# Triangular inverses of a chunked RWKV-7 scan: 64x64 matrices in two passes, or their diagonal 32x32 blocks in one

## The chip, the cores and the metric

The kernel runs on one NeuronCore of a Trainium2 chip. The metric is the device time in microseconds (us) of one execution, as the median of several. TensorE is called PE for its products and PEld for its weight loads, VectorE is DVE, ScalarE is ACT, GpSimd is POOL, SyncE is SP. All operands of the part that is changed are float32.

## The reference

Two layers on a sequence of 256 tokens with 1024 features: an RWKV-7 time mix, then a sparse attention, each followed by a squared-ReLU MLP. The change touches only the recurrence of the time mix:

```
def wkv7_scan(r, w, k, v, a, b):
    """S_t = S_{t-1} diag(w_t) + (S_{t-1} a_t) b_t^T + v_t k_t^T ;  y_t = S_t r_t."""
    def step(S, inp):
        r_t, w_t, k_t, v_t, a_t, b_t = inp
        sa = jnp.einsum('bhij,bhj->bhi', S, a_t)
        S = S * w_t[:, :, None, :] + sa[..., None] * b_t[:, :, None, :] + v_t[..., None] * k_t[:, :, None, :]
        return S, jnp.einsum('bhij,bhj->bhi', S, r_t)
```

There are 16 heads of 64 features. The kernel does the recurrence in 4 chunks of 64 tokens. In a chunk the values `u_t = S_{t-1} a_t` depend on one another through a strictly lower triangular 64x64 matrix N (entry s,t is the product of a_s and b_t, with the decays in both), so that they are found with the inverse of (I - N). For 16 heads and 4 chunks that is 64 inverses of 64x64 matrices.

## The kernel before, in words

Everything is in one block per engine, written out by hand; each engine runs its instructions in the order of the code, and semaphores (`inv_pe0`, `inv_dve0`, `inv_act0`, `inv_pool0` and the same with 1) tie them together. The weights of the linears stream from HBM through a ring of four slots (`raw`), are split into a high and a low part by ACT (L1120) and DVE (L1526), and are multiplied by PE in `unit_mm` (L451).

The part around the change is this:

- PE ends the linear "v" (`linear8`, L620), transposes V into `ps` (L625) and the third chunk of BK (`b_k(2)`, L609). ACT copies the first half of the transposed V into `UV` (L1277) and then `BKT` (L1267), DVE the other half (L1701).
- The inverses follow. A pair of heads lies on the 128 partitions, one head on each half (`at(e)`), so the 64 matrices are 32 pairs. They are done in two passes (`NPAIR`) of two streams (s = 0 and 1) of 8 pairs (`NP_`); a stream's 8 pairs of 64x64 matrices are 128 partitions by 512 columns, one PSUM bank, and while one stream's result is copied, PE works on the other stream.
- In a pass, N comes from a product of AR and BK (`lower_products`, L658); ACT copies it to `Lr`; DVE masks its 16x16 diagonal blocks (L1737), turns them over in blocks of 32x32 (L1740) and adds the identity (L1742). POOL masks out of `Lr` what lies between the 16x16 blocks of a 32x32 block (`E32`) and between the two 32x32 blocks (`E64`, L2132).
- Then `times` (L667) makes one product for each matrix on 64x64 tiles of the PE array: sq1, sq2, add2, sq3, add3, add4 build the inverse of the 16x16 blocks as (I + N)(I + N^2)(I + N^4)(I + N^8); m32a and m32b join them to inverses of 32x32 blocks, m64a and m64b those to the 64x64 inverse `Rinv`. ACT copies the products that are used as they are (L1284), DVE adds the others to the running product (`add_to_product`, L1729) and turns over what becomes the next left factor (`turn_over`, L1732).
- While DVE prepares sq1, PE runs products whose result nobody reads (`idle_products`, L675: 4 before each stream's sq1, 5 at the end of the last pass). Then come `g_products` (L644), which DVE masks into `Gs` (L1711), and the recurrence over the four chunks, in which `Rinv` is the left factor of L815.

Of the kernel before, what the change touches and what calls it, by code (L numbers as in the profile page):

```python
# [8 lines left out]
P = 128  # L9
# [10 lines left out]
SUB = 16  # L20
LD, LI, LG = 64, 64, 160
# [19 lines left out]
def constants():  # L41
# [3 lines left out]
    t = np.arange(C)[None, :]  # L45
    same = (s // SUB) == (t // SUB)
    same32 = (s // (2 * SUB)) == (t // (2 * SUB))
    tt = np.arange(C)[None, :]
    cols = {
# [46 lines left out]
for _n, _w in (("ident", P), ("mean", P), ("pair", P), ("center", P), ("gmask", 2 * C), ("lmask16", C), ("lmask32", C),  # L96
               ("lmask64", C), ("eye64", C), ("hsel", 3 * H - 2), ("chunk", T),
               ("dist", P * TT * (TT + 1) // 2), ("adc", TT * H * 16), ("unit", P), ("shift", P), ("last", 2)):
    CONST_AT[_n] = (_o, _w)
    _o += _w  # L100
# [3 lines left out]
def rwkv_nsa_trunk(nc, t, out):  # L104
# [79 lines left out]
    LT = [place(f"LT{n}", [P, NP_, C], off(12 + n, 4096)) for n in range(2)]  # L184
    E32 = [place(f"E32{n}", [P, NP_, C], off(14 + n)) for n in range(2)]
    E64 = [place(f"E64{n}", [P, NP_, C], off(14 + n, 4096)) for n in range(2)]

    INV = {"L": 1, "sq1": 2, "sq2": 3, "add2": 4, "sq3": 5, "add3": 6, "add4": 7, "m32a": 8, "m32b": 9,  # L190
           "m64a": 10, "m64b": 11}
    NINV, NDVE, NACT, NPOOL = 11, 13, 5, 2
    Lr = [place(f"Lr{n}", [P, NP_, C], off(6, 2048 * n)) for n in range(2)]
# [126 lines left out]
    with ctx:  # L320
# [99 lines left out]
        def _(pe):  # L420
# [201 lines left out]
            pe.wait_ge(ev_act, EV0["v"] + 4)  # L622
            for q in range(TT):
                for k in range(FT):
                    last = nc.tensor.transpose(ps[:, 2 * q + k // 4, (k % 4) * P:(k % 4 + 1) * P],  # L625
                                               V[:, k, q * P:(q + 1) * P], cc("ident"))
                last.then_inc(sem("vT"), 1)
            pe.wait_ge(sem("bkt_act"), 1)
            b_k(2)

            pe.wait_ge(sem("ar_ready"), 2)

# [15 lines left out]
            def inv_bank(s, pair, name):  # L648
                return 4 * s + (NINV * pair + INV[name] - 1) % 4

            def lower_products(s, pair):

                p0 = (2 * pair + s) * NP_
                bank = inv_bank(s, pair, "L")
                for p in range(NP_):
                    k, c = (p0 + p) // NCH, p % NCH
                    for e in range(2):
                        last = mm(ps[at(e), bank, p * C:(p + 1) * C], AR[at(e), k, c, 0, :], BK[at(e), k, c, 0, :],  # L658
                                  start=True, stop=True)
                last.then_inc(sem(f"inv_pe{s}"), 1)  # L660

            def times(s, pair, name, lhs, which):

                bank = inv_bank(s, pair, name)
                for p in range(NP_):
                    for e in range(2):
                        last = mm(ps[at(e), bank, p * C:(p + 1) * C], lhs[s][at(e), p, :], DP[s][at(e), p, which, :],  # L667
                                  start=True, stop=True)
                last.then_inc(sem(f"inv_pe{s}"), 1)


# [5 lines left out]
            both = range(2)  # L677
            for pair in range(NPAIR):

                def dve_did(s, n):  # L680
# [1535 lines left out]
```

## Time and profile before

| | |
|---|---|
| time, median of 3 runs | 781.61 us (779.17, 781.61, 781.89) |
| span of the profiled execution, first to last instruction | 774.2 us |
| what lies around the span (median less span) | 7.4 us |
| PE busy | 745.7 us, 96% of the span, 7876 matmul records |
| PEld busy | 700.5 us, 90% |
| DVE busy | 521.3 us, 67% |
| ACT busy | 380.7 us, 49% |
| POOL busy | 71.4 us, 9% |
| mean granted clock of TensorE | 0.991 |

The profile gives no time of its own for the profiled execution beside its span. A float32 product is two records of PE and two of PEld (16 products of `times` are 32 records). Where the chain of waits puts the end on an engine, the time is that engine's; busy time elsewhere costs nothing by itself. A matmul record holds the whole way of its data through the array, so that records of a stream overlap; what a stream takes per record is its length, less one record's time, through the number of records.

### The profile page before, as it was taken

The page shows a single profiled execution, that of the slowest core. Times are in us where ns is not written, and L with a number is a line of the kernel's source. Part 1 is how long each engine was busy: PE and PEld are TensorE (multiplying, and loading weights), DVE is VectorE, ACT ScalarE, POOL GpSimd, SP SyncE. Part 2 cuts the span into 40 slices and gives each one's busy share as a digit, 9 for nine tenths or more (in the row PEclk, how much of TensorE's full clock was granted, in tenths as well). Part 3 has the DMA queues.
Part 4 walks back from the last instruction along what each step waited for, and adds up shares of the span by engine and source line. Part 5 has one row for each costly group of instructions (what it writes and reads, how often), then busy time and mean ns, then how long its engine had stood idle before and what let it go on. Part 6 is the DMA issues. An engine that isn't in the chain of part 4 may idle for free.

```text
span 774.2 us, 18656 instructions
## 1 busy us (share of the span) xinstructions
PE 745.7 (96%) x7876; PEld 700.5 (90%) x7876; DVE 521.3 (67%) x742; ACT 380.7 (49%) x584; POOL 71.4 (9%) x52
## 2 busy tenths in 40 slices
PE   8999999998999999999999999989999999999997
PEld 6988888998878999999999989866579999999997
DVE  4896986776453788785555678686857977764441
ACT  6657453121443645544444435767866544443441
POOL 0000005190130000000000010024320000000000
PEclk9999999999999999999999999998999999999999
DMA  9954330000111589967666554400045665676651
GB/s 294 273 172 130 108 110 3 5 3 2 57 56 45 164 216 250 241 193 221 197 195 194 170 164 115 159 1 1 1 139 164 193 209 178 204 212 194 192 164 54
DMA packets 110893, 109.23 MB, mean 141 GB/s; under 512 B 7120, under 2 KB 109776, under 8 KB 110704
## 3 DMA queue, kind: packets, MB, share of 16 engines
q1 hardware_dynamic: 110832, 108.34, 47.1%
q8 instruction: 47, 0.77, 0.4%
q14 instruction: 14, 0.11, 0.0%
HBM read 107.28 MB, written 1.05 MB: 140 GB/s over the span
## 4 chain that ended last, share of the span: by engine, by line
PE 83%; DVE 8%; ACT 3%; SPq 2%; DMA 1%; issue 1%; POOL 1%; ACTq 0%; DVEq 0%; POOLq 0%
PE ps L451 63%; PE ps L667 4%; DVE SB L2053 1%; DMA raw<-in_rwkv_w_in 1%; DVE Gs L1711 1%; PE ps L815 1%; ACT SB L1458 1%; PE ps L764 1%; PE ps L566 1%; PE ps L978 1%; DVE nmx L2059 1%; PE ps L758 1%; DVE LT L1737 1%; PE ps L549 1%; POOL t L2122 1%
## 5 line engine op out<-in xcount | busy, mean ns | idle before, releaser
L1526 DVE TENSOR_TENSOR wlo<-raw,whi 128x1024 fp32r<-128x1024 f32 x188 | 226.1, 1225 | 88.4 <-ACT whi L1120 86.1
L1120 ACT ACTIVATE whi<-raw 128x1024 fp32r<-128x1024 f32 x124 | 130.4, 1059 | 127.8 <-PE ps L451 122.4
L451 PE MATMUL ps<-xh,whi 128*128 128x256 f32 x896 | 178.6, 281 | 2.6 <-DVE xl L2081 1.0
L451 PE MATMUL ps<-xl,whi 128*128 128x256 f32 x896 | 175.7, 278 | 0.0
L451 PE MATMUL ps<-xh,wlo 128*128 128x256 f32 x896 | 175.6, 278 | 0.0
L451 PEld LDWEIGHTS ps<-xh,whi 128*128 128x128 f32 x896 | 135.7, 188 | 6.7 <-issue 4.1
L451 PEld LDWEIGHTS ps<-xl,whi 128*128 128x128 f32 x896 | 135.5, 188 | 0.0
L451 PEld LDWEIGHTS ps<-xh,wlo 128*128 128x128 f32 x896 | 135.4, 188 | 0.0
L1355 ACT ACTIVATE whi<-raw 128x1024 fp32r<-128x1024 f32 x64 | 68.0, 1063 | 78.0 <-PE ps L451 59.4
L451 PE MATMUL ps<-hh,whi 128*128 128x256 f32 x512 | 99.8, 276 | 0.0
L451 PE MATMUL ps<-hh,wlo 128*128 128x256 f32 x512 | 99.8, 276 | 0.0
L451 PE MATMUL ps<-hl,whi 128*128 128x256 f32 x512 | 99.8, 276 | 0.0
L451 PEld LDWEIGHTS ps<-hh,whi 128*128 128x128 f32 x512 | 77.1, 188 | 0.0
L451 PEld LDWEIGHTS ps<-hh,wlo 128*128 128x128 f32 x512 | 77.0, 188 | 0.0
L451 PEld LDWEIGHTS ps<-hl,whi 128*128 128x128 f32 x512 | 77.0, 188 | 0.0
L1863 DVE SCALAR_TENSOR_TENSOR rl<-ps,ri 128x512 f32<-128x512 f32 x32 | 22.1, 691 | 30.3 <-PE ps L451 29.9
L667 PEld LDWEIGHTS ps<-DP,LT 64*64 64x64 f32 x1024 | 30.7, 135 | 3.7 <-DVE DP L1742 2.5
L667 PE MATMUL ps<-DP,LT 64*64 64x64 f32 x1024 | 31.8, 219 | 1.8 <-DVE DP L1729 0.9
L2175 POOL TENSOR_TENSOR SB<-SB,cof 128x512 f32<-128x512 f32 (+1 forms) x16 | 24.4, 1523 | 80.0 <-DVE cof L2075 79.9
L1562 DVE TENSOR_TENSOR h<-h,ps 128x512 f32<-128x512 f32 x16 | 11.0, 688 | 29.8 <-PE ps L451 27.0
L1284 ACT ACTIVATE DP<-ps 128x512 f32<-128x512 f32 x16 | 9.6, 597 | 35.8 <-PE ps L667 35.8
L1866 DVE TENSOR_TENSOR s<-rl 128x512 f32<-128x512 f32 x32 | 22.2, 692 | 1.1
(309 smaller groups left out, 988.0 us busy)
## 6 DMA issues: line engine op xcount, KB each, us to landing
raw<-in_mlp_w SPq DMA_DIRECT2D x128, 512.0 KB, 4.4
raw<-in_rwkv_w_in SPq DMA_DIRECT2D x24, 512.0 KB, 5.0
raw<-in_nsa_w_in SPq DMA_DIRECT2D x20, 512.0 KB, 4.5
raw<-in_rwkv_w_out SPq DMA_DIRECT2D x8, 512.0 KB, 3.5
raw<-in_nsa_w_out SPq DMA_DIRECT2D x8, 512.0 KB, 3.5
cw<-in_nsa_cmp_w SPq DMA_DIRECT2D x4, 512.0 KB, 9.4
cst<-in_consts SPq DMA_DIRECT2D x1, 1047.0 KB, 11.2
xtok<-in_x SPq DMA_DIRECT2D x2, 512.0 KB, 4.3
```

The source lines that it names most:

```text
L451: last = mm(ps[:, bank0 + m, 0:T], w[:, slot, c0:c0 + P], x_[:, kk, :], start=(kk == 0 and n == 0), stop=(kk == ktiles - 1 and n == 2))
L549: last = mm(ps[:, 4 + 2 * (k % 2) + i, 0:T], lup[half, k * P:(k + 1) * P], hwa[half, :], start=True, stop=True)
L566: last = mm(ps[0:width, bank, 0:T], ldown[:, k, c0:c0 + width], mixg[:, k, :], start=(k == 0), stop=(k == FT - 1))
L667: last = mm(ps[at(e), bank, p * C:(p + 1) * C], lhs[s][at(e), p, :], DP[s][at(e), p, which, :], start=True, stop=True)
L1120: A(whi[:, s, :], raw[:, s, :], ACT.Copy).then_inc(hi_ready, 1)
L1284: A(dst, ps[:, bank, :].rearrange("p (k n) -> p k n", n=C), ACT.Copy).then_inc(sem(f"inv_act{s}"), 1)
L1355: A(whi[:, 2 * gg + j, :], raw[:, 2 * gg + j, :], ACT.Copy).then_inc(hi_ready, 1)
L1526: v.tensor_tensor(wlo[:, slot, :], raw[:, slot, :], whi[:, slot, :].bitcast(f32), ALU.subtract)\
L1562: v.tensor_tensor(h[:, 2 * g:2 * g + 2, :], h[:, 2 * g:2 * g + 2, :], ps[:, 2 * (g % 2):2 * (g % 2) + 2, 0:T], ALU.add).then_inc(ev_dve, 1)
L1863: v.scalar_tensor_tensor(rl[:, gg, :, :], ps[:, 2 * gg:2 * gg + 2, 0:T], 0.0, normal(2), ALU.max, ALU.mult)\
L1866: v.tensor_tensor(s2[:, gg, :, :], rl[:, gg, :, :], rl[:, gg, :, :], ALU.mult).then_inc(sem("s2_ready"), 1)
L2175: g.tensor_tensor(x, x, cof[:, q, b, 4 * j:4 * j + 4].unsqueeze(2).broadcast_to([P, 4, w]), ALU.mult)\
```

## The change

Each 64x64 matrix is no longer kept whole. Of a matrix only the two 32x32 blocks on its diagonal go through the steps up to m32b; the block below the diagonal (`F`) is made by a product of its own and is only used in m64a. The two heads of a pair have four diagonal blocks, one on each quarter of the 128 partitions. A stream is now 16 pairs (`NP_`) of 32 columns, again 128 partitions by 512 columns and one bank, and two streams hold all 32 pairs, so there is one pass.

- `times` makes four products of 32x32 for a pair where it made two of 64x64. m64a and m64b are two products for a pair (`moves`).
- A product of BK and AR gives the transposed matrix (`U`), so that DVE masks both orientations straight out of PSUM (`inv_first`) and the first turning-over is gone. `E64` and POOL's mask for it are gone.
- `Rinv` is put together from its parts: ACT copies the upper left block and m64b of the first head, DVE the lower right block and m64b of the second, POOL writes the zeros.
- The first stream's L, U and F come before the transposes of V. PE writes the third BK chunk's transposes to banks 0 and 1, and ACT's queue takes the first stream's copies between the others. `idle_products` stay only at the end (4 of them).

```diff
-        "lmask16": (s > t) & same,
-        "lmask32": (s > t) & ~same & same32,
-        "lmask64": (s > t) & ~same32,
-        "eye64": s == t,
+        "lmask16": (r > j) & same,
+        "umask16": (r < j) & same,
+        "lmask32": (r > j) & ~same,
+        "eye32": r == j,
...
-    NP_ = 8
-    NPAIR = FT * NCH // NP_ // 2
-    DP = [place(f"DP{n}", [P, NP_, 2, C], off(12 + n)) for n in range(2)]
...
-    NINV, NDVE, NACT, NPOOL = 11, 13, 5, 2
-    Lr = [place(f"Lr{n}", [P, NP_, C], off(6, 2048 * n)) for n in range(2)]
+    NP_ = FT * NCH // 2
+
+    DP = [place(f"DP{n}", [P, 2, NP_, Q], off(12 + n)) for n in range(2)]
+    LT = [place(f"LT{n}", [P, NP_, Q], off(12 + n, 4096)) for n in range(2)]
+    E32 = [place(f"E32{n}", [P, NP_, Q], off(14 + n)) for n in range(2)]
+    Lr = [place(f"Lr{n}", [P, NP_, Q], off(14 + n, 2048)) for n in range(2)]
+    F64 = [place(f"F64{n}", [P, NP_, Q], off(14 + n, 4096)) for n in range(2)]
+
+
+    INV = {"L": 1, "U": 2, "F": 3, "sq1": 4, "sq2": 5, "add2": 6, "sq3": 7, "add3": 8, "add4": 9, "m32a": 10, "m32b": 11,
+           "m64a": 12, "m64b": 13}
+    INV_ACT = {"L": 1, "F": 2, "sq1": 3, "sq2": 4, "m32a": 5, "own": 7, "m64a": 8, "m64b": 9}
+    INV_DVE = {"lower": 1, "upper": 2, "first": 3, "sq1T": 4, "sq2T": 5, "add2": 6, "sq3T": 7, "add3": 8, "add4": 9, "add4T": 10,
+               "m32b": 11, "m32bT": 12, "own": 14, "m64b": 15}
...
+            def inv_bank(s, name):
+                return 4 * (1 - s) + (INV[name] + 2 * s - 1) % 4
+
+            def quad(n):
+                return slice(Q * n, Q * n + Q)
+
+            def inv_inputs(s, name):
+
+                bank = inv_bank(s, name)
                 for p in range(NP_):
-                    k, c = (p0 + p) // NCH, p % NCH
+                    k, c = (s * NP_ + p) // NCH, p % NCH
                     for e in range(2):
-                        last = mm(ps[at(e), bank, p * C:(p + 1) * C], AR[at(e), k, c, 0, :], BK[at(e), k, c, 0, :],
+                        a, b = AR[at(e), k, c, 0, :], BK[at(e), k, c, 0, :]
+                        if name == "F":
+                            last = mm(ps[quad(2 * e + 1), bank, p * Q:(p + 1) * Q], a[:, quad(1)], b[:, quad(0)], start=True, stop=True)
+                            continue
+                        for r in range(2):
+                            lhs, rhs = (a, b) if name == "L" else (b, a)
+                            last = mm(ps[quad(2 * e + r), bank, p * Q:(p + 1) * Q], lhs[:, quad(r)], rhs[:, quad(r)],
+                                      start=True, stop=True)
+                last.then_inc(sem(f"inv_pe{s}"), 1)
+
+            def times(s, name, lhs, which, moves=((0, 0), (1, 1), (2, 2), (3, 3))):
+
+                bank = inv_bank(s, name)
+                for p in range(NP_):
+                    for n, m in moves:
+                        last = mm(ps[quad(m), bank, p * Q:(p + 1) * Q], lhs[s][quad(n), p, :], DP[s][quad(n), which, p, :],
                                   start=True, stop=True)
                 last.then_inc(sem(f"inv_pe{s}"), 1)
...
+            pe.wait_ge(sem("ar_ready"), 2)
+            pe.wait_ge(sem("bkt_act"), 1)
+            pe.wait_ge(sem("bkt_dve"), 1)
+            for name in ("L", "U", "F"):
+                inv_inputs(0, name)
+            pe.wait_ge(ev_act, EV0["v"] + 4)
+            for q in range(TT):
+                for k in range(FT):
+                    last = nc.tensor.transpose(ps[:, 2 * q + k // 4, (k % 4) * P:(k % 4 + 1) * P],
+                                               V[:, k, q * P:(q + 1) * P], cc("ident"))
+                last.then_inc(sem("vT"), 1)
+            dve_did(0, "upper")
+            times(0, "sq1", LT, 0)
+            pe.wait_ge(sem("v_copied"), 2)
+            for k in range(FT):
+                last = nc.tensor.transpose(ps[:, k // 4, (k % 4) * P:(k % 4 + 1) * P], BK[:, k, 2, :, :], cc("ident"))
+            last.then_inc(sem("bkT"), 1)
+            pe.wait_ge(sem("bkt_dve"), 3)
+            inv_inputs(1, "L")
+            inv_inputs(1, "U")
+            pe.wait_ge(sem("bkt_act"), 2)
+            inv_inputs(1, "F")
+
...
-                    idle_products(inv_bank(s, pair, "sq1"), 4)
-                    dve_did(s, 3)
-                    times(s, pair, "sq1", LT, 0)
...
-            idle_products(inv_bank(0, NPAIR - 1, "m64a"), 5)
-            for s in range(2):
-                pe.wait_ge(sem(f"inv_dve{s}"), NDVE * NPAIR)
+            for s in both:
+                if s:
+                    dve_did(s, "upper")
+                    times(s, "sq1", LT, 0)
+                act_did(s, "sq1")
+                dve_did(s, "sq1T")
+                times(s, "sq2", LT, 0)
+                times(s, "add2", LT, 1)
+            for s in both:
+                act_did(s, "sq2")
+                dve_did(s, "sq2T")
+                times(s, "sq3", LT, 0)
+                dve_did(s, "add2")
+                times(s, "add3", LT, 1)
+            for s in both:
+                dve_did(s, "add3")
+                times(s, "add4", LT, 1)
+            for s in both:
+                dve_did(s, "add4")
+                pe.wait_ge(sem(f"inv_pool{s}"), 1)
+                times(s, "m32a", E32, 1)
+            for s in both:
+                act_did(s, "m32a")
+                dve_did(s, "add4T")
+                times(s, "m32b", LT, 0)
+            for s in both:
+                dve_did(s, "m32b")
+                times(s, "m64a", F64, 1, ((1, 0), (3, 2)))
+            for s in both:
+                act_did(s, "m64a")
+                dve_did(s, "m32bT")
+                times(s, "m64b", LT, 0, ((0, 0), (2, 2)))
+
+            idle_products(inv_bank(1, "m64a"), 4)
+            for s in both:
+                act_did(s, "m64b")
+                dve_did(s, "m64b")
+            pe.wait_ge(sem("rinv_zero"), 2)
...
+            act.wait_ge(sem("inv_dve0"), INV_DVE["lower"])
+            inv_copy(0, "L", Lr[0][:, :, :])
+            inv_copy(0, "F", F64[0][:, :, :])
...
+            act.wait_ge(sem("inv_dve0"), INV_DVE["first"])
+            inv_copy(0, "sq1", DP[0][:, 0, :, :])
+            bkt_copy(2, 0)
+            inv_copy(1, "L", Lr[1][:, :, :])
+            inv_copy(1, "F", F64[1][:, :, :])
+            act.wait_ge(sem("inv_dve1"), INV_DVE["first"])
+            inv_copy(1, "sq1", DP[1][:, 0, :, :])
...
+                    inv_copy(s, name, DP[s][:, 0, :, :])
+            for s in range(2):
+                act.wait_ge(sem(f"inv_dve{s}"), INV_DVE["m32b"])
+                pairs_ = slice(s * NP_, (s + 1) * NP_)
+                for e in range(2):
+                    rows = slice(HD * e, HD * e + Q)
+                    A(Rinv[rows, pairs_, 0:Q], DP[s][rows, 1, :, :], ACT.Copy).then_inc(sem(f"inv_act{s}"), 1)
+                inv_copy(s, "m64a", DP[s][:, 0, :, :])
+            for s in range(2):
+                inv_copy(s, "m64b", Rinv[0:Q, s * NP_:(s + 1) * NP_, Q:C], slice(0, Q))
+
...
+            def inv_first(s):
+                done, power, prod = sem(f"inv_dve{s}"), DP[s][:, 0, :, :], DP[s][:, 1, :, :]
+                v.tensor_tensor(LT[s][:, :, :], inv_out(s, "L"), each("lmask16"), ALU.mult).then_inc(done, 1)
+                v.tensor_tensor(power, inv_out(s, "U"), each("umask16"), ALU.mult).then_inc(done, 1)
+                after(s, "upper")
+                v.tensor_tensor(prod, power, each("eye32"), ALU.add).then_inc(done, 1)
...
+            inv_first(0)
             dve.wait_ge(sem("vT"), 2)
             for n in range(2):
                 v.tensor_copy(UV[HD:P, 2 + n, :].rearrange("p (b n) -> p b n", b=2),
                               ps[HD * n:HD * n + HD, 2:4, :]).then_inc(sem("bkt_dve"), 1)
+            after_act(0, "sq1")
+            turn_over(0, DP[0][:, 0, :, :])
+            inv_first(1)
+            after_act(1, "sq1")
+            turn_over(1, DP[1][:, 0, :, :])
+            for s in range(2):
+                dve.wait_ge(sem(f"inv_pe{s}"), INV["add2"])
+                after_act(s, "sq2")
+                turn_over(s, DP[s][:, 0, :, :])
+                after(s, "first")
+                add_to_product(s, "add2")
+            for s in range(2):
+                dve.wait_ge(sem(f"inv_pe{s}"), INV["add3"])
+                turn_over(s, inv_out(s, "sq3"))
+                after(s, "add2")
+                add_to_product(s, "add3")
+            for s in range(2):
+                after(s, "add3")
+                add_to_product(s, "add4")
+                after(s, "add4")
+                turn_over(s, DP[s][:, 1, :, :])
+            for s in range(2):
+                add_to_product(s, "m32b")
+                after(s, "m32b")
+                turn_over(s, DP[s][:, 1, :, :])
+                for e in range(2):
+                    rows = slice(HD * e + Q, HD * e + 2 * Q)
+                    v.tensor_copy(Rinv[rows, s * NP_:(s + 1) * NP_, Q:C], DP[s][rows, 1, :, :]).then_inc(sem(f"inv_dve{s}"), 1)
+            for s in range(2):
+                rows = slice(HD, HD + Q)
+                v.tensor_copy(Rinv[rows, s * NP_:(s + 1) * NP_, Q:C], inv_out(s, "m64b", rows)).then_inc(sem(f"inv_dve{s}"), 1)
...
+            for e in range(2):
+                g.memset(Rinv[HD * e + Q:HD * e + 2 * Q, :, 0:Q], 0.0).then_inc(sem("rinv_zero"), 1)
+            pool.wait_ge(sem("rinv_zero"), 2)
...
+            for s in range(2):
+                pool.wait_ge(sem(f"inv_act{s}"), INV_ACT["L"])
+                g.tensor_tensor(E32[s][:, :, :], Lr[s][:, :, :], cc("lmask32").unsqueeze(1).broadcast_to([P, NP_, Q]), ALU.mult)\
+                    .then_inc(sem(f"inv_pool{s}"), 1)
```

The two streams of instructions on PE, from the end of linear "v" on. Rows name the line in their own kernel, the operation, what is written and read (`ps` is PSUM; `DP_99`, `LT_101` belong to stream 0, `DP_100`, `LT_102` to stream 1), the output's shape and how many follow one another. In the kernel before, up to sq2 and add2 of the first pass:

```order
L625 MATMUL ps<-cst,V 128x128 x16
L609 MATMUL ps<-cst,BK 128x128 x8
L658 MATMUL ps<-BK,AR 64x64 x32
L675 MATMUL ps<-cst 128x256 x4
L667 MATMUL ps<-DP_99,LT_101 64x64 x16
L675 MATMUL ps<-cst 128x256 x4
L667 MATMUL ps<-DP_100,LT_102 64x64 x16
L667 MATMUL ps<-DP_99,LT_101 64x64 x32
L667 MATMUL ps<-DP_100,LT_102 64x64 x32
```

After the change, the same place:

```order
L658 MATMUL ps<-BK,AR 32x32 x64
L658 MATMUL ps<-AR,BK 32x32 x64
L654 MATMUL ps<-BK,AR 32x32 x32
L690 MATMUL ps<-cst,V 128x128 x16
L667 MATMUL ps<-DP_99,LT_101 32x32 x64
L697 MATMUL ps<-cst,BK 128x128 x8
L658 MATMUL ps<-BK,AR 32x32 x64
L658 MATMUL ps<-AR,BK 32x32 x64
L654 MATMUL ps<-BK,AR 32x32 x32
L667 MATMUL ps<-DP_99,LT_101 32x32 x128
L667 MATMUL ps<-DP_100,LT_102 32x32 x192
```

The products of the inputs moved ahead of the transposes of V, a step has 64 products where it had 16, and the fillers between the steps are gone.

On DVE, after the change, from m32b to the masks of G:

```order
L1742 TENSOR_TENSOR DP_99<-DP_99,ps 128x512
L1745 STREAM_TRANSPOSE LT_101<-DP_99 128x512
L1779 COPY Rinv<-DP_99 32x16x32 x2
L1742 TENSOR_TENSOR DP_100<-DP_100,ps 128x512
L1745 STREAM_TRANSPOSE LT_102<-DP_100 128x512
L1779 COPY Rinv<-DP_100 32x16x32 x2
L1782 COPY Rinv<-ps 32x16x32 x2
L1791 TENSOR_TENSOR Gs_97<-ps,cst 128x512 x8
```

Two copies of stream 0 into `Rinv` stand ahead of stream 1's addition, which PE's m64a of stream 1 waits for. Before, the addition of stream 1 stood right behind the turning-over of stream 0.

## Rows read from the trace of the kernel before

**Rows 1.** The page's shares of the chain that ended last, by engine and line.

```profile
PE 83%; DVE 8%; ACT 3%; SPq 2%; DMA 1%; issue 1%; POOL 1%; ACTq 0%; DVEq 0%; POOLq 0%
```

**Rows 2.** Chain of waits, pieces from 118.5 to 205 us: start us, us, what.

```profile
119.30 4.54 POOL t L2122
...
130.28 8.64 PE ps L667 x288
...
156.89 8.64 PE ps L667 x288
...
176.05 2.36 PE ps L675 x10
178.40 1.12 PE ps L644 x16
...
189.94 3.17 PE ps L815 x15
...
199.76 1.89 PE ps L815 x16
```

**Rows 3.** Timeline of PE: start us, us, operation, out<-in, shapes, xcount of records.

```profile
119.18 1.97 PE L625 MATMUL ps<-cst,V 128*128 128x128 f32 x16 [0.69 <-ACT V L1193]
120.98 1.04 PE L609 MATMUL ps<-cst,BK 128*128 128x128 f32 x8
122.58 2.38 PE L658 MATMUL ps<-BK,AR 64*64 64x64 f32 x64 [0.55 <-ACT UV L1277]
124.89 1.99 PE L675 MATMUL ps<-cst 128*128 128x256 f32 x8
126.92 1.15 PE L667 MATMUL ps<-DP,LT 64*64 64x64 f32 x32
...
130.28 9.55 PE L667 MATMUL ps<-DP,LT 64*64 64x64 f32 x320 [0.28 <-DVE DP L1742]
```

**Rows 4.** Timeline of PE again, products on quarters of the array (L513, L1027).

```profile
496.40 1.10 PE L513 MATMUL ps<-qss,cst 128*32 128x64 f32 x64
...
498.08 0.32 PE L1027 MATMUL ps<-cst,qrt 32*64 32x32 f32 x8
```

**Rows 5.** Groups by line and form, 118.5 to 178.3 us: busy us, mean ns | idle before.

```profile
L667 PE MATMUL ps<-DP,LT 64*64 64x64 f32 x1024 | 31.8, 219 | 1.8 <-DVE DP L1729 0.9 <-DVE DP L1742 0.9
...
L2132 POOL TENSOR_TENSOR E<-Lr,cst 128x512 f32<-128x512 f32 x8 | 13.6, 1723 | 20.6 <-ACT Lr L1284 20.6
L1732 DVE STREAM_TRANSPOSE LT<-DP 128x512 f32<-128x512 f32 x16 | 11.4, 710 | 5.0 <-ACT DP L1284 2.5 <-PE ps L667 2.2
L1729 DVE TENSOR_TENSOR DP<-DP,ps 128x512 f32<-128x512 f32 x16 | 10.4, 663 | 2.9 <-PE ps L667 2.9
...
L1284 ACT ACTIVATE DP<-ps 128x512 f32<-128x512 f32 x16 | 9.6, 597 | 35.8 <-PE ps L667 35.8
...
L1742 DVE TENSOR_TENSOR DP<-DP,cst 128x512 f32<-128x512 f32 x4 | 3.6, 903 | 0.1
...
L1701 DVE COPY UV<-ps 64x1024 f32<-64x1024 f32 x2 | 2.4, 1223 | 4.3 <-PE ps L625 4.3
...
L1277 ACT ACTIVATE UV<-ps 64x1024 f32<-64x1024 f32 x2 | 2.0, 1018 | 1.3 <-PE ps L625 1.2
```

**Rows 6.** Busy time by stretch: us, PE PEld DVE ACT POOL (x), PEclk, DMA, GB/s.

```profile
118.50:178.30 59.80, 56.30 (x1474) 52.34 (x1474) 40.07 (x54) 15.60 (x24) 34.28 (x15) 1.00 0.01 3
186.40:189.20 2.80, 0.00 (x0) 0.00 (x0) 2.80 (x5) 0.38 (x1) 0.00 (x0) 1.00 0.00 0
189.90:193.30 3.40, 3.40 (x23) 3.40 (x23) 0.43 (x1) 1.91 (x3) 0.00 (x0) 0.50 0.00 0
227.50:230.90 3.40, 2.53 (x15) 1.75 (x14) 2.92 (x4) 0.89 (x3) 1.27 (x1) 0.99 0.40 110
230.90:234.30 3.40, 3.26 (x20) 2.56 (x20) 1.89 (x4) 1.72 (x4) 0.00 (x0) 0.50 0.14 49
```

**Rows 7.** DMA queues in 118 to 180 us: packets, MB, share of 16 engines.

```profile
q8 instruction: 12, 0.20, 1.3%
```

More of the change, by code:

```diff
@@ L179, in rwkv_nsa_trunk @@
     Gs = [place(f"Gs{n}", [P, FT, NCH, 2 * C], off([14, 12][n])) for n in range(2)]
-    NP_ = 8
-    NPAIR = FT * NCH // NP_ // 2
-    DP = [place(f"DP{n}", [P, NP_, 2, C], off(12 + n)) for n in range(2)]
[L184 to L191, printed above, removed]
-    NINV, NDVE, NACT, NPOOL = 11, 13, 5, 2
-    Lr = [place(f"Lr{n}", [P, NP_, C], off(6, 2048 * n)) for n in range(2)]
+    NP_ = FT * NCH // 2
[9 more added lines that the diff above has]
+               "m32b": 11, "m32bT": 12, "own": 14, "m64b": 15}
     Rinv = place("Rinv", [P, FT * NCH, C], off(3))
@@ L675, in idle_products @@
                     mm(ps[:, bank, 0:T], cc("ident"), cc("chunk"), start=True, stop=True)
-            both = range(2)
-            for pair in range(NPAIR):
-                def dve_did(s, n):
-                    pe.wait_ge(sem(f"inv_dve{s}"), NDVE * pair + n)
-                def act_did(s, n):
-                    pe.wait_ge(sem(f"inv_act{s}"), NACT * pair + n)
-                def pool_did(s, n):
-                    pe.wait_ge(sem(f"inv_pool{s}"), NPOOL * pair + n)
-                for s in both:
-                    if pair:
-                        act_did(s, 0)
-                    elif s == 0:
-                        pe.wait_ge(sem("v_copied"), 2)
-                    else:
-                        pe.wait_ge(sem("bkt_act"), 2)
-                        pe.wait_ge(sem("bkt_dve"), 3)
-                    lower_products(s, pair)
-                for s in both:
-                    idle_products(inv_bank(s, pair, "sq1"), 4)
-                    dve_did(s, 3)
-                    times(s, pair, "sq1", LT, 0)
-                for s in both:
-                    act_did(s, 2)
-                    dve_did(s, 4)
-                    times(s, pair, "sq2", LT, 0)
-                    times(s, pair, "add2", LT, 1)
-                for s in both:
-                    act_did(s, 3)
-                    dve_did(s, 5)
-                    times(s, pair, "sq3", LT, 0)
-                    dve_did(s, 6)
-                    times(s, pair, "add3", LT, 1)
-                for s in both:
-                    dve_did(s, 8)
-                    times(s, pair, "add4", LT, 1)
-                for s in both:
-                    dve_did(s, 9)
-                    pool_did(s, 1)
-                    times(s, pair, "m32a", E32, 1)
-                for s in both:
-                    act_did(s, 4)
-                    dve_did(s, 10)
-                    times(s, pair, "m32b", LT, 0)
-                for s in both:
-                    dve_did(s, 11)
-                    pool_did(s, 2)
-                    times(s, pair, "m64a", E64, 1)
-                for s in both:
-                    act_did(s, 5)
-                    dve_did(s, 12)
-                    times(s, pair, "m64b", LT, 0)
```

134 lines of the change are left out of this document (36 added, 98 removed).

## The prediction, as it was recorded before the changed kernel was run

> **What bounds the kernel now.** I read the page's shares of the chain first: PE holds 83% of it [rows 1], so outside the part that is changed the kernel runs at PE's pace, and time taken out there comes off the end one for one. Then the chain of waits around the change [rows 2] and PE's timeline [rows 3]. Linear "v" ends at 118.5 us (119.18 less the 0.69 that PE sat idle) and the first product of G starts at 178.3 to 178.4: that is 59.8 us for the transposes and 64 inverses. In it PE is busy for 56.3 us, DVE for 40.1, ACT for 15.6, POOL for 34.3, at the full granted clock [rows 6]. The reader is to see in [rows 2] that the two passes read alike, 26.6 us apart (130.28 and 156.89): each has one long piece of PE, and short pieces of DVE and PE in turns. PE's busy time in there includes products that nobody reads, so part of it is waiting in disguise: 2 us before each stream's sq1 [rows 3] and 2.36 us at the end [rows 2].
>
> **The pace of a product.** Here the sum is decided. 320 records of 64x64 products take 9.55 us; less one record's 0.22 [rows 5] that is 29.2 ns each, or 58.5 ns for the two tiles in use [rows 3]. 64 records on four quarters of the array's columns, also 64 columns wide, take 1.10 us, or 14.0 ns each, 56 ns for the four [rows 4]. So a tile takes a record of 64 columns every 56 to 58 ns, and tiles work beside one another, two or four. With 32 columns I expect half of that for each tile and a few ns of start, 29 to 32 ns for four records. The trace has no stream of 32x32 products: L1027 has 8 records on four row quarters in 0.32 us, (0.32 - 0.23) / 7 = 13 ns each, in which most is its filling [rows 4]. The bounds for a record are thus 7.3 ns (29.2 / 4) and 29.2 ns (tiles give nothing). I take 8.0, because both streams above are explained by columns alone. A product step of a stream is then 64 products, 128 records, 1.02 us; F, m64a and m64b use two tiles and have 64 records, 0.98 us.
>
> **The change, part by part, on PE's queue after 118.5 us.** Two streams make 20 full steps (L, U, sq1, sq2, add2, sq3, add3, add4, m32a, m32b): 20 x 1.02 = 20.4. Six half steps: 5.9. Three groups of 8 transposes at 0.9 [rows 3]: 2.6. The fillers at the end, 8 records at 1.99 / 8 and less [rows 3]: 1.8. Together 30.7 us.
>
> Then what PE waits for. I laid the other queues beside it with DVE's sum and turning-over at 0.66 and 0.71, its identity addition at 0.90, its copies of V at 1.22, ACT's copy at 0.60 and its V copies at 1.02 [rows 5], and 0.26 us from a stream's last record to the next engine's start.
> - 0.5 us for ACT's second V copy, before PE may write the third BK chunk's transposes into banks 0 and 1; 0.4 us for DVE's second V copy, before stream 1's L. What is queued behind these two waits is all of stream 1, and stream 0's sq2 too; DVE's mask of stream 1 waits with them.
> - 1.6 us after stream 1's sq1: ACT's copy 0.60, DVE's turning-over 0.71, the hand-over 0.26.
> - 0.7 us before stream 1's add4 (DVE has four operations between).
> - 1.6 us before stream 1's m64a: DVE does two copies of stream 0 into Rinv (0.6 each; ACT's copy of 512 columns takes 0.60, DVE's sum 0.66 [rows 5]) before the sum that PE waits for.
> - Elsewhere the other stream's step hides the hand-over. The last copies into Rinv (two of 0.6) lie beside the fillers.
> Waits: 4.8 us. A step also has a slower first turn through the array; 26 steps at 0.03 make 0.8. Sum 30.7 + 4.8 + 0.8 = 36.3 us, so G starts at 154.8 instead of 178.3: 23.5 us less.
>
> Where it comes from: one pass less takes 26.6 us away; U, F and the four-fold number of products give a little back; and the start of the first stream no longer stands behind the transposes and POOL's 4.54 us on t, which is on the chain today [rows 2] because ACT's copy to Lr waits for it.
>
> What I cost at nothing: POOL loses six of its eight masks of 1.72 us [rows 5] and gains two memsets before V is there; its E32 masks end near 130.5 and are needed at 143.7, its fold of t and its zeros for U at 147 and 136, before PE gets there at 154.8. If the masks were late, they would cost up to 1.7 us each. DVE's and ACT's work is off the path but for the waits above. The constants shrink by 64 columns, before the stretch, hidden behind nothing that the chain shows; 0.
>
> After G nothing is changed; weights come through a ring of four slots that is full there (DMA busy 1% [rows 6]), so the rest shifts as it is. Instruction fetches in this stretch are 12 packets of 16 KB [rows 7]; twice the products in 36 us instead of 60 would be some 24, one in 1.5 us, still little.
>
> The sum by the trace: 774.2 - 23.5 = 750.7 us of span, and with the 7.4 us around it 758.1; since 7.4 is how the median of the runs stands to the span, that is 781.6 - 23.5 as well.
>
> **A rule that speaks against it.** [Rows 4] show records of one engine starting 14.0 ns apart on the average, on different tiles, over 64 records. The Trainium skill, TensorE: Matmul & The Clock Gate, section "Wait — 56ns, not 53.3ns?", says that matmuls never start less than about 25 ns apart however small they are. By the trace that floor can't hold across tiles; for one tile it would change nothing, since mine has 29 to 32 ns. Should it hold for a long stream, a step would be 128 x 25 = 3.2 us, and my layout then gives G at 198, 20 us later than before: about 801 us, an estimate from that page. The fourth rival below is its case, priced from rows.
>
> **Rivals.**
> 1. A step is bound by what feeds PE, or by two tiles at a time: 14.0 or 14.6 ns a record (the fastest long pace that the trace shows, and half of 29.2). For it: nothing faster is shown over more than eight records, and each product is now a quarter of the work for the same four instructions. Against: 14.0 is just what 64 columns take. A step is then 1.8 to 1.9 us, PE has no waits but 3 us, G starts at 167.5 to 169: 10 us less, 771 us.
> 2. The clock. It is full throughout the stretch now; it fell to 0.50 for 3.4 us at 189.9, after 2.8 us in which PE did nothing, and at 230.9, after a stretch with PE busy 2.53 of 3.4 us [rows 6]. At 0.50, 15 records of L815 take 3.17 us, and 16 take 1.89 at full clock [rows 2]. The fillers between the steps are gone, and two waits of 1.6 us come. Two or three such falls inside the inverses would cost up to 1.7 us each: 762 us. All of the stretch at half clock is the first rival's price.
> 3. The gain is there but PE waits more: DVE's queue is strictly ordered and POOL runs beside it at the start (DVE's addition from SBUF alone takes 0.90 us where one from PSUM takes 0.66 [rows 5]; my layout has 0.9 us of slack there). 1 to 2 us; it lies in the forecast's own range.
> 4. Slower: small products gain nothing from the tiles. A stream of 32x32 has 1472 products against 704, 2.1 times. If a record takes as long as now, 29.2 ns, a step is 3.7 us and G starts at 210.6, 32 us later: 814 us. It decides from 18 ns a record on (a step of 2.3 us), where the gain is gone; between 18 and 29 lie 782 to 814. For it: four times as many instructions per unit of work, from one queue. Against: [rows 4].
> That the change doesn't do what it says would show as idle PE between the steps of two streams; the queues above say how long those waits are.
>
> **How the numbers follow.** Forecast 758, own range 753 (7.3 ns, no slow start) to 763 (10 ns): 46%. Rival 1, 764 to 776: 27%. Rival 2, 760 to 766: 13%. Rival 4: 11%, of it 3% near no change. Anything else: 3%. What can be told from no change is 0.5%, 3.9 us. Faster by more than that: 0.46 + 0.27 + 0.13, less a little, 0.85; within it 0.05; slower 0.10. The range for 8 in 10 is 752 to 776.
>
> **What would show it.** Right: 128 records of a step in 1.1 to 1.3 us, G starting 22 to 25 us earlier, PE idle 1.3 to 1.7 us before stream 1's sq2 and m64a, the clock at 1.00 over the stretch. Wrong: a step of 1.8 us or more (rivals 1 and 4, told apart by 14 or over 18 ns a record); granted clock of 0.50 in the stretch (rival 2); or the gain in the stretch and lost again between G and the first record of "o0".

## The result, and the profile after

| | before | after |
|---|---|---|
| time, median | 780.39 us (777.00 to 781.89) | 802.85 us (799.38 to 809.97) |
| span of the profiled execution | 774.2 us | 797.3 us |
| linear "v" ends | 118.5 us | 119.99 us |
| first product of G | 178.4 us | 206.00 us |
| stretch between the two | 59.8 us | 86.0 us |
| from the first product of G to the end | 595.8 us | 591.3 us |
| instruction fetches in the stretch | 12 packets | 24 packets |

The changed kernel is slower: ratio 1.030, 95% interval 1.023 to 1.037. The forecast was 758 us, range 752 to 776, so it was wrong, in sign too. The difference of 23.1 us in the spans is 26.2 in the changed stretch, 1.5 more before it and 4.5 less behind it (each rounded). The 1.5 go with a fall of the clock to 0.50 for 3.4 us at 11 us, where the kernel before had 1.00. The 4.5 go with the clock behind G: the kernel before had 0.50 there for 3.4 us twice [rows 6] and for 6.8 us more from 521.3 on, the changed one for 3.4 us at 256.6 only, and 10.2 us less at half speed are worth up to 5.1. So neither has to come from the work of the inverses. Of the traces used below, that of experiment 1 is of an execution longer than the others of its kernel (821.46 us against 806.27 to 812.3), so its stretch is an upper figure.

The page's shares of the chain, against [rows 1], and one of its groups (busy us, mean ns, then the idle time before them and what ended it):

```profile
PE 86%; DVE 6%; issue 5%; ACT 2%; DMA 1%; ACTq 0%; SPq 0%; DVEq 0%
...
L667 PE MATMUL ps<-DP,LT 32*32 32x32 f32 x1920 | 30.9, 234 | 22.2 <-issue 20.6
```

"issue" is the new name on the chain, 5% where it was 1%: PE is idle, and it waits for nothing that the profile shows. PE's timeline against [rows 3] (start us, us, operation, idle before in brackets):

```profile
119.99 1.26 PE L658 MATMUL ps<-BK,AR 64*32 64x32 f32 x126
...
121.10 0.67 PE L658 MATMUL ps<-AR,BK 64*32 64x32 f32 x54
124.17 0.80 PE L658 MATMUL ps<-AR,BK 64*32 64x32 f32 x71 [2.40 <-issue]
...
128.18 0.32 PE L654 MATMUL ps<-BK,AR 64*32 64x32 f32 x8 [2.31 <-issue]
...
142.73 1.93 PE L667 MATMUL ps<-DP,LT 32*32 32x32 f32 x128 [1.18 <-issue]
146.20 1.93 PE L667 MATMUL ps<-DP,LT 32*32 32x32 f32 x128 [1.53 <-issue]
149.66 1.51 PE L667 MATMUL ps<-DP,LT 32*32 32x32 f32 x96 [1.53 <-issue]
152.78 2.35 PE L667 MATMUL ps<-DP,LT 32*32 32x32 f32 x159 [1.61 <-DVE LT L1745]
156.72 1.93 PE L667 MATMUL ps<-DP,LT 32*32 32x32 f32 x128 [1.59 <-issue]
160.61 1.93 PE L667 MATMUL ps<-DP,LT 32*32 32x32 f32 x128 [1.97 <-issue]
...
181.97 1.93 PE L667 MATMUL ps<-DP,E 32*32 32x32 f32 x127 [1.42 <-issue]
185.30 1.54 PE L667 MATMUL ps<-DP,E 32*32 32x32 f32 x98 [1.41 <-issue]
...
199.97 2.88 PE L667 MATMUL ps<-DP,LT 32*32 32x32 f32 x100 [0.28 <-issue]
...
202.78 3.28 PE L673 MATMUL ps<-cst 128*128 128x256 f32 x8
```

Two things are to be seen. The pace that the forecast rests on is there: (1.26 - 0.20) / 125 = 8.5 ns a record. But after each 128 records PE stops. The records start again at 142.73, 146.20 and 149.66, 3.46 us apart, and a little later 3.33 us apart (181.97, 185.30) or 3.89 (156.72, 160.61). From 124.17 to 199.97 there are 21 such blocks of 128 records, 3.61 us each on the average. 128 records of PE and their 128 weight loads are 256 instructions.

The queue of instruction fetches from 118 to 207 us, against [rows 7] (packets, MB, share of 16 engines):

```profile
q8 instruction: 24, 0.39, 1.8%
```

Windows at the start, up to the fall of the clock, behind it, and from G to the end (span, busy us and count of PE, PEld, DVE, ACT, POOL, granted clock, DMA share, GB/s):

```profile
10.90:14.30 3.40, 3.40 (x12) 2.86 (x11) 0.84 (x1) 0.82 (x2) 0.00 (x0) 0.50 1.07 395
119.99:140.50 20.51, 11.49 (x782) 10.50 (x783) 7.34 (x8) 6.05 (x8) 8.38 (x6) 1.00 0.02 4
140.60:205.40 64.80, 39.00 (x2199) 36.20 (x2193) 21.48 (x25) 8.35 (x14) 15.01 (x4) 0.50 0.02 5
206.00:797.30 591.30, 571.07 (x5487) 543.27 (x5486) 391.95 (x560) 294.03 (x463) 35.74 (x31) 1.00 0.50 149
```

In the second and third row PE is busy for 56 to 60% of the time. The clock halved between them, and the blocks came no more slowly: the four from 124.17 to 139.39 are 3.81 us apart on the average, at full clock, and the fifteen from 142.73 to 196.25 are 3.57 us apart, at half clock.

### The profile page after: what moved, and what is told of

It is laid out like the page before. It is cut to its first block, busy times and chain, and to the rows that moved or that the text cites. A ratio compares the mean times of both kernels' runs of the same rounds, so it can differ in the third digit from the quotient of the medians.

```text
span 797.3 us, 21618 instructions
## 1 busy us (share of the span) xinstructions
PE 737.0 (92%) x9378; PEld 692.6 (87%) x9378; DVE 510.3 (64%) x720; ACT 379.4 (48%) x582; POOL 62.5 (8%) x48
## 4 chain that ended last, share of the span: by engine, by line
PE 86%; DVE 6%; issue 5%; ACT 2%; DMA 1%; ACTq 0%; SPq 0%; DVEq 0%
PE ps L453 64%; PE ps L667 5%; DVE SB L2082 1%; DVE Gs L1791 1%; PE ps L771 1%; PE ps L822 1%; PE ps L985 1%; PE ps L568 1%; PE ps L1004 1%; DMA xtok<-in_x 1%; PE ps L658 1%; PE ps L484 1%; PE ps L974 1%; DVE nmx L2088 1%; PE ps L765 1%
## 5 line engine op out<-in xcount | busy, mean ns | idle before, releaser
L453 PE MATMUL ps<-xh,whi 128*128 128x256 f32 x896 | 178.3, 280 | 1.3 <-DVE xl L2110 1.0
L667 PE MATMUL ps<-DP,LT 32*32 32x32 f32 x1920 | 30.9, 234 | 22.2 <-issue 20.6
L667 PEld LDWEIGHTS ps<-DP,LT 32*32 32x32 f32 x1920 | 28.5, 148 | 24.4 <-issue 22.6
L1892 DVE SCALAR_TENSOR_TENSOR rl<-ps,ri 128x512 f32<-128x512 f32 x32 | 22.1, 691 | 30.2 <-PE ps L453 29.8
L1279 ACT ACTIVATE DP<-ps 128x512 f32<-128x512 f32 x8 | 4.7, 596 | 49.0 <-PE ps L667 49.0
```

What stands on the lines that cost most here:

```text
L453: last = mm(ps[:, bank0 + m, 0:T], w[:, slot, c0:c0 + P], x_[:, kk, :], start=(kk == 0 and n == 0), stop=(kk == ktiles - 1 and n == 2))
L667: last = mm(ps[quad(m), bank, p * Q:(p + 1) * Q], lhs[s][quad(n), p, :], DP[s][quad(n), which, p, :], start=True, stop=True)
L1892: v.scalar_tensor_tensor(rl[:, gg, :, :], ps[:, 2 * gg:2 * gg + 2, 0:T], 0.0, normal(2), ALU.max, ALU.mult)\
```

## The experiments

Theory A: PE's instructions arrive in blocks of 256 (16 KB), one in 3.4 to 3.5 us, and a product in float32 is four of them. Theory B: small tiles of the array are slow to feed. Theory C: the low clock. A fourth explanation was tried too, that the idle time is a wait for VectorE's and ScalarE's steps that the profile shows badly.

**1. The kernel before, with twice the instructions.** Each product is cut into two of 64x32, which work beside one another; layout, passes and the other engines' work stay.

```diff
-                        last = mm(ps[at(e), bank, p * C:(p + 1) * C], lhs[s][at(e), p, :], DP[s][at(e), p, which, :],
-                                  start=True, stop=True)
+                        for r in range(2):
+                            last = mm(ps[HD * e + 32 * r:HD * e + 32 * r + 32, bank, p * C:(p + 1) * C],
+                                      lhs[s][at(e), p, 32 * r:32 * r + 32], DP[s][at(e), p, which, :], start=True, stop=True)
```

> The kernel before, with each 64x64 product of the inverses made as two products of 64x32 on two column tiles: the same two passes, the same copies, the same array work per step (64 records at the 14.0 ns of L513 are 0.90 us, 32 at 29.2 are 0.93), but twice the instructions. Theory A (instructions come in blocks of 256 that take 3.4 to 3.5 us each, one at a time, and a float32 product is four of them): 640 more products are 2560 more instructions, 10 more blocks at 3.46 us; the stretch from linear v to G goes from 60 us to about 60 + 27 = 87, since the old blocks ran at 3.74 us: 24 us slower or more, 802 to 812, PE idle by issue of 1.5 to 2.5 us in each period of 3.5. Theory B (the array or the queue behind it is slow with 32x32 tiles alone): no change, 780. Theory C (the half clock of the new kernel makes the loss): no change, 780, or a loss only where the clock falls.

Measured: 810.86 us, ratio to before 1.034 (1.028 to 1.039). PE's timeline, and the clock in two windows of the stretch:

```profile
141.45 1.99 PE L668 MATMUL ps<-DP,LT 64*32 64x64 f32 x128 [1.36 <-issue]
145.35 1.86 PE L668 MATMUL ps<-DP,LT 64*32 64x64 f32 x114 [1.91 <-issue]
147.69 0.42 PE L668 MATMUL ps<-DP,LT 64*32 64x64 f32 x14 [0.49 <-DVE DP L1730]
149.09 0.91 PE L668 MATMUL ps<-DP,LT 64*32 64x64 f32 x49 [0.97 <-issue]
```

```profile
140.00:160.00 20.00, 10.76 (x644) 9.59 (x636) 8.48 (x13) 1.79 (x3) 0.00 (x0) 1.00 0.02 5
160.00:180.00 20.00, 14.84 (x638) 13.03 (x638) 9.58 (x12) 4.18 (x7) 12.84 (x8) 1.00 0.02 4
```

The old algorithm, with little but its instructions doubled, loses as much as the changed one and shows the same stops, in both windows at the full clock. The whole time is inside the 802 to 812 us expected. Its first product of G starts at 211.19, 91.8 us after linear v, where about 87 were expected. That is theory A; the 32x32 tiles and the new layout aren't needed for the loss, nor is the low clock.

**2. The changed kernel, with the clock held up.** Three products of 256 columns that nobody reads stand ahead of each of the 20 product steps.

```diff
+                for n in range(3):
+                    mm(ps[:, bank, 0:T], cc("ident"), cc("chunk"), start=True, stop=True)
```

> The changed kernel with three products of 256 columns, that nobody reads, in front of each product step: 12 more instructions a step, 1.3 us more of PE work, put there to keep the clock up. Theory A (blocks of instructions): the clock goes to full or nearly, the period of 3.46 us for 256 instructions stays, 216 more instructions are one more block, so the time is 800 to 808, no faster than the changed kernel. Theory C (half clock is the cause): records of a step from 15 to 8.3 ns, 18 steps in the slow stretch win 0.85 us each and pay 1.3 us partly in idle time: 785 to 795.

Measured: 811.95 us, 4 us above the 800 to 808 that theory A expected; ratio to before 1.039 (1.033 to 1.044), where the changed kernel's is 1.030. Its rows from PE's timeline, and a window:

```profile
146.02 1.29 PE L669 MATMUL ps<-DP,LT 32*32 32x32 f32 x128
147.23 1.56 PE L666 MATMUL ps<-cst 128*128 128x256 f32 x6
148.73 0.26 PE L669 MATMUL ps<-DP,LT 32*32 32x32 f32 x8
150.00 1.22 PE L669 MATMUL ps<-DP,LT 32*32 32x32 f32 x120 [1.00 <-issue]
```

```profile
152.80:211.10 58.30, 48.83 (x1896) 38.82 (x1896) 13.54 (x22) 6.67 (x11) 2.17 (x1) 0.97 0.02 4
```

With the clock at 0.97 from 152.8 us on nothing was won. Six records of fillers hold PE for 1.49 to 1.50 us (147.23 to 148.73), so the 20 groups are 30 us of work at the full clock, and they made the stretch only 6.6 us longer (118.5 to 211.1, 92.6 us, against 86.0). Most of them went into time in which PE would have stood still. A stop is shorter behind a filler, 1.00 us here, since the next block goes on arriving meanwhile. Theory C is out as the cause. The low clock costs little in the changed kernel, since 128 records take 1.93 us at it and their block 3.46. It shows in the fillers ahead of G, 3.28 us at 202.78 against 1.99 in [rows 3].

**3 and 4. The same 256 small products, written out and as a loop.** Both stand in the kernel before, ahead of G, where nothing else runs beside them. They are 1024 instructions of 32x32 tiles, written out in experiment 3, and as four turns over 64 products in experiment 4.

```diff
+            def probe():
+                for p in range(16):
+                    for n in range(4):
+                        r = slice(32 * n, 32 * n + 32)
+                        mm(ps[r, 0, p * 32:(p + 1) * 32], cst[r, 32 * n:32 * n + 32], cst[r, 32 * n:32 * n + 32],
+                           start=True, stop=True)
+
+            for _ in range(4):
+                probe()
```

Experiment 4 has `with pe.Fori(0, 4) as i:` in place of the `for`: a loop that PE turns itself.

> The kernel before, and between the inverses and G 256 more products of 32x32 on four tiles, in a row, of constants, written out (1024 instructions, 4 blocks), to measure the stream by itself. Theory A: 4 blocks at 3.46 us less what is already fetched, 11 to 14 us more in the profile, in bursts of 1.1 us with gaps of 2.3. Theory B (pace of the array at 8.3 ns a record): 4.3 us more.

> The same 256 products of 32x32 as four turns of a loop over 64 products: the same records, but only one block of instructions to fetch, then it lies in the instruction memory. Theory A: one gap of up to 3.5 us, then turns of 1.1 us and some 0.4 us for the branch: 6 to 9 us more than the kernel before, at least 4 us less than the unrolled one. Theory B: as the unrolled one, and the branches on top.

PE's timeline of the products written out:

```profile
178.06 2.15 PE L741 MATMUL ps<-cst 32*32 32x32 f32 x233
182.34 1.93 PE L741 MATMUL ps<-cst 32*32 32x32 f32 x128 [2.13 <-issue]
185.80 1.93 PE L741 MATMUL ps<-cst 32*32 32x32 f32 x128 [1.54 <-issue]
189.26 0.54 PE L741 MATMUL ps<-cst 32*32 32x32 f32 x23 [1.53 <-issue]
189.73 2.50 PE L644 MATMUL ps<-AR,BK 64*128 64x128 f32 x20
```

And of the loop:

```profile
177.91 5.53 PE L741 MATMUL ps<-cst 32*32 32x32 f32 x512
183.43 7.42 PE L644 MATMUL ps<-AR,BK 64*128 64x128 f32 x128
```

This pair decides it. The same products on the same data take 11.7 us from the first to G's start written out, and 5.5 us as a loop, without a stop. Written out, the first 233 records run at (2.15 - 0.23) / 232 = 8.3 ns; from then on each block of 128 records starts 3.46 us after the one before. No engine but PE is in it, and the array does the same work in both, so neither theory B nor a hidden wait is left for these stops. The clock is not the same in both: it is 0.50 from 182.3 us on in experiment 3 and 1.00 throughout the loop. That lengthens a block's records from 1.1 to 1.93 us, which still end 1.5 us before the next block, so it doesn't make the stops. The loop's records come out at (5.53 - 0.23) / 511 = 10.4 ns; the turns themselves are in that. It did better than theory A expected of it, 6 to 9 us with one stop.

The queue of instruction fetches shows the same. From 170 to 195 us, written out and as a loop:

```profile
q8 instruction: 6, 0.10, 1.6%
```

```profile
q8 instruction: 4, 0.07, 1.0%
```

And in experiment 3 from 182 to 186 us, in 40 slices of 0.1 us, around the block that starts at 182.34:

```profile
GB/s 0 0 0 0 0 0 0 0 0 0 0 0 0 0 164 0 0 0 0 0 0 0 0 0 0 0 0 0 0 0 0 0 0 0 0 0 0 0 0 0
q8 instruction: 1, 0.02, 1.5%
```

One packet starts in the slice from 183.4 us, 1.1 us after the block has started. It takes 1.5% of 16 x 4 us, about 0.96 us, and the next block starts at 185.80, 1.4 us after it has landed. In the changed kernel the block of 142.73 has its packet in the slice from 143.8, and the next block starts at 146.20. So the 3.46 us are a round of one fetch at a time: 1.1 us until its packet starts, 1 us of packet, 1.4 us until PE goes on. That the start of one block is what asks for the next is the plain reading of these distances; no run was made for it. The two ran once each (796.3 and 793.0 us), and the whole times aren't compared, only the stretch.

**5. The changed kernel, with 1024 instructions fewer and the same columns.** sq2 and add2 have the same left factor, and so have sq3 and add3. Each pair becomes one product of 64 columns per tile; DP is laid out so that both right factors lie side by side, and the results fill two banks.

```diff
+            def times_both(s, name):
+                bank = inv_bank(s, name)
+                for p in range(NP_):
+                    for n in range(4):
+                        b_, c0 = bank + p // 8, (p % 8) * 2 * Q
+                        m_ = mm(ps[quad(n), b_, c0:c0 + 2 * Q], LT[s][quad(n), p, :], DP[s][quad(n), p, :, :], start=True, stop=True)
...
-                times(s, "sq2", LT, 0)
-                times(s, "add2", LT, 1)
+                times_both(s, "sq2")
...
-                times(s, "sq3", LT, 0)
...
-                times(s, "add3", LT, 1)
+                times_both(s, "sq3")
```

> The changed kernel with sq2 and add2 made as one product of 64 columns for each 32x32 block (they have the same left factor), and sq3 and add3 too: 256 of the 1472 small products go, which is 1024 of the 5888 instructions of TensorE in the stretch, while the columns that the array works through stay the same. Theory A (TensorE's instructions arrive in blocks of 256, one in 3.4 to 3.5 us, whatever is in them): 4 blocks fewer, 4 x 3.46 = 13.8 us less than the changed kernel: about 789 us, with gaps of about 1.5 to 2.5 us after each block still there. A filler theory (the stops are waits for VectorE's and ScalarE's steps, badly shown): those steps stay, so 800 to 803. A theory that the array's pace sets it (columns): 0 to 2 us less, 800 to 803. Theory C (clock): unchanged, 800 to 803.

Measured: 789.16 us (786.11 to 790.6), ratio to before 1.013 (1.008 to 1.017), which is 13.7 us less than the changed kernel, and still a little slower than the kernel before. Four blocks at 3.46 us are 13.8, as expected; the stretch became 14.0 us shorter (72.0 against 86.0). PE's timeline, from the merged products to G, and the fetches from 118 to 192 us:

```profile
146.72 6.29 PE L677 MATMUL ps<-DP,LT 32*32 32x64 f32 x286 [1.65 <-DVE LT L1760]
154.91 1.55 PE L677 MATMUL ps<-DP,LT 32*32 32x64 f32 x97 [1.90 <-issue]
...
158.37 1.28 PE L667 MATMUL ps<-DP,LT 32*32 32x32 f32 x128 [1.64 <-issue]
162.11 1.54 PE L667 MATMUL ps<-DP,LT 32*32 32x32 f32 x98 [2.46 <-issue]
...
190.55 8.14 PE L635 MATMUL ps<-AR,BK 64*128 64x128 f32 x128
```

```profile
q8 instruction: 20, 0.33, 1.8%
```

The array works through as many columns as in the changed kernel, and the other engines do the same steps; 20 packets are left of 24, and the time went with them. So the array's pace doesn't set it, and the hidden waits for other engines don't either.

**6. Whole products, but one pass.** What the change wanted, without its price in instructions: the kernel before with its 704 products of 64x64, all four groups of 8 pairs as streams of one pass, two and two in turn, no fillers between the steps, and the first two lower products ahead of the transposes of v. Where PE would wait for one pair of streams, the other has a step.

```diff
+    ORDER = [("A", "sq1"), ("B", "L"), ("A", "s2"), ("B", "sq1"), ("A", "s3"), ("B", "s2"), ("A", "add4"), ("B", "s3"), ("A", "m32a"),
+             ("B", "add4"), ("A", "m32b"), ("B", "m32a"), ("A", "m64a"), ("B", "m32b"), ("A", "m64b"), ("B", "m64a"), ("B", "m64b")]
+    GRP_S = {"A": (0, 1), "B": (3, 2)}
...
+            lower_products(0)
+            lower_products(1)
...
-            for pair in range(NPAIR):
+            for grp, what in ORDER:
+                for s in GRP_S[grp]:
+                    step_of(s, what)
```

> Of the kernel before, whole 64x64 products stay (704, four instructions each), but all four groups of 8 pairs run as four streams in one pass, two and two in turn, without the unread products between steps; the first two groups' lower products come ahead of the transposes of v. Theory A: 704 products are 11 blocks of 256 instructions; at 58.4 ns a product a block lasts 3.74 us, just above the 3.46 us that a block takes to arrive, so the products keep their pace and only waits go: about 47 to 50 us instead of 59.8 between linear v and the first G product, and about 769 us in all (760 to 777). A rival: TensorE's clock falls or the steps of the streams wait on VectorE and ScalarE, whose work is the same as before: no gain, 779 to 783. If any launching of small products with gaps after each 256 instructions shows here too, 790 or more.

Measured: 771.65 us (768.57 to 775.19), ratio to before 0.991 (0.987 to 0.994), inside the 760 to 777 expected. It is the only one of these kernels that beats the one before, by a small margin, 0.9%. PE's timeline:

```profile
118.04 2.08 PE L654 MATMUL ps<-BK,AR 64*64 64x64 f32 x64
120.06 1.97 PE L684 MATMUL ps<-cst,V 128*128 128x128 f32 x16
123.36 1.09 PE L689 MATMUL ps<-cst,BK 128*128 128x128 f32 x8 [1.34 <-ACT UV L1286]
125.72 1.97 PE L663 MATMUL ps<-DP,LT 64*64 64x64 f32 x32 [1.27 <-DVE DP L1735]
129.07 1.98 PE L663 MATMUL ps<-DP,LT 64*64 64x64 f32 x32 [1.38 <-DVE DP L1735]
131.58 3.68 PE L654 MATMUL ps<-BK,AR 64*64 64x64 f32 x64 [0.53 <-DVE UV L1759]
135.05 19.24 PE L663 MATMUL ps<-DP,LT 64*64 64x64 f32 x640
...
172.94 7.42 PE L644 MATMUL ps<-AR,BK 64*128 64x128 f32 x128
```

From 135 us on PE doesn't stop once: 640 records of 0.22 us at (19.24 - 0.22) / 639 = 29.8 ns. G starts at 172.94, 54.9 us after linear v, where 47 to 50 were expected; four waits of 4.5 us together at the start and a clock of 0.50 there (64 records in 3.68 us, where 2.08 do at 118.04) are what is left over. At 64 products of 59.6 ns, a block of 256 instructions lasts 3.8 us, a little above the 3.46 us in which the next one comes.

The stretches side by side. Instructions are the records of PE and PEld in a window over the stretch; of each kernel the fetches are those of its stretch.

| kernel | instructions | packets | stretch, us | us a packet |
|---|---|---|---|---|
| before | 2948 | 12 | 59.8 | 5.0 |
| four streams | 2881 | 11 | 54.9 | 5.0 |
| merged products | 4958 | 20 | 72.0 | 3.6 |
| changed | 5980 | 24 | 86.0 | 3.6 |
| changed, with fillers | 6194 | 24 | 92.6 | 3.9 |
| before, products split | 5514 | 22 | 91.8 | 4.2 |

In the first two PE's own work or waits take longer than the fetches. In the others a packet costs 3.6 us or more. The split kernel is above that, and its 4.2 is an upper figure; that the waits of its two passes come on top of the fetches would fit, and wasn't tried by itself.

## Why the prediction was wrong

**The step that failed** is the one that read the instruction fetches: "Instruction fetches in this stretch are 12 packets of 16 KB [rows 7]; twice the products in 36 us instead of 60 would be some 24, one in 1.5 us, still little." The count was right, 24 packets came. "Still little" was wrong. It judged the queue by its share (1.3%, of sixteen engines) and its bytes, and neither is its limit: one block is fetched after another for PE, and the row says nothing of how fast the next may follow. The experiments show 3.46 us where nothing else holds PE up, and the changed kernel 3.33 to 4.01, more than twice the 1.5 that the forecast needed. A packet of 1 us in 3.46 is 1.8% of sixteen engines, so the share that the changed kernel shows was already all that this way of fetching gives. 24 x 3.46 = 83 us, and the stretch took 86.0. The forecast said 36.3.

The kernel before held a warning that could be worked out. Its long stream [rows 3] takes 58.5 ns a product; 64 products, 256 instructions, are 3.74 us. So its long stream ran just above the fetch's limit (3.46), and no row showed code supplied faster over several blocks. The row that spoke for more, 64 records at 14.0 ns in [rows 4], is 128 instructions, half a block, which can have arrived before. A short burst can't show the pace at which code is supplied.

**What held.** The pace of a record: taken at 8.0 ns, bounds 7.3 to 29.2, measured 8.3 to 8.8 at the full clock. 126 and 128 records take 1.26 and 1.29 us, the first sign that the forecast named. The passes fell from two to one, and DVE is busy for 28.9 us from 118.5 to 206, where it was 40.1 [rows 6]. Of PE's waits for other engines, the one after stream 1's sq1 is 1.61 us (the record at 152.78), where 1.6 was expected. It is the only one that the profile shows; the others that were worked out, 3.2 us together, don't show beside the stops, so the runs don't test them. After G nothing was lost.

**The rivals.** The second one, the clock, came true and beyond: 0.50 from 140.6 to 205.4 us, not for two or three spells of 3.4 us but for three quarters of the stretch; all of it the forecast called "the first rival's price", 771. But it isn't what cost the time, as experiments 1 and 2 show: with the clock at 1.00 and at 0.97 PE still stops after each 256 instructions. The first rival spoke of "what feeds PE" but priced it at 14.0 or 14.6 ns a record, from the short burst; the average of the stretch is 3.46 / 128 = 27 ns. The fourth, with 11% and up to 814 us, had the right sign and nearly the price (803), and even the right word for it, "four times as many instructions per unit of work, from one queue". Its mechanism was wrong: the tiles do give their gain, record by record. A fifth rival, the supply of code, was missing, although it follows from the count of instructions.

**Two rules weighed.** The forecast weighed a floor of about 25 ns between starts of matmuls (the Trainium skill, TensorE: Matmul & The Clock Gate, "Wait — 56ns, not 53.3ns?") against the trace and set it aside. The runs bear that out across tiles: 233 records on four tiles start 8.3 ns apart, which is 33 ns for one tile, so that a floor for one tile isn't tested. The average of 27 ns lies near that floor by chance, since the loop of experiment 4 goes at 10.4 ns.

The Trainium skill, Runtime: NRT & Kernel Launch, section "Instruction fetch mechanics", says that each engine's instruction memory is filled in blocks of 16 KiB, 256 instructions, the next page being fetched while the current one runs, and that this is hidden by the rate at which instructions are issued. The size agrees with these runs (0.39 MB in 24 packets, a stop after each 128 records and their weight loads). That it is hidden holds for the kernel before and not for the changed one.

## What to carry to other kernels

Count instructions of each stretch as well as columns and records: here a float32 product is four instructions of TensorE, straight code came in at 256 in about 3.46 us, and in a long straight stream a product that keeps the array busy for less than 54 ns (3.46 us / 64) was paid as 54 ns or a little more. Splitting products onto smaller tiles pays only if it doesn't raise the number of instructions, or if the code is a loop that is there already. When a change asks a resource for a higher rate, look for a row in which that rate was kept up for long enough; a small share of it isn't room.

## What the runs showed of the hardware

- PE's code arrives in blocks of 256 instructions, one in 3.46 us in straight code when nothing else holds PE up (the starts 182.34, 185.80 and 189.26 of experiment 3), and one in 3.33 to 4.01 us, 3.61 on the average, in the changed kernel. By bytes 3.46 us is 4.7 GB/s, but the packet itself takes 1 us of it; what the 1.1 us before and the 1.4 us behind it go into isn't shown. The period didn't follow PE's clock.
- 233 records, with their weight loads 466 instructions, ran before the first stop of experiment 3. That fits the rest of one block (105 records) and the whole of the next (128).
- A loop over 256 instructions ran its four turns without a stop, at 10.4 ns a record with the turns.
- Products in float32 on four 32x32 tiles start 8.3 ns apart on the average at the full clock, and (1.93 - 0.24) / 127 = 13.3 ns at 0.50.
- The granted clock fell to 0.50 after 20.5 us of stops in which PE was busy for 56%, and stayed there over 65 us of the same pattern. In experiment 1, busy for 54% of the 20 us from 140 on, it stayed at 1.00. What tells these apart remains open.
- A profile can give the same stop two names. In the split kernel, "issue" and a wait for DVE stand side by side; only the period of 256 instructions shows which ones are fetches.
